# A two-layer attention and convolution trunk: attention turns one step later behind the scores, four score buffers, and one weight unit in another slot

## The chip, the cores and the metric

The kernel runs on one core of a Trainium2 chip, in one launch, in float32 with split products (below). The metric is the device time of the launch in microseconds. Before the change it is 2429.41 us, the median of three runs (2428.79 to 2430.34).

## The reference

Two layers, each on a residual stream x of 1024 positions by 1024 channels:

```
h    = rmsnorm(x);  proj = h @ w_in
q, k, v, conv_in = split(proj)            # 8 heads of 64; 512 + 512 convolution columns
q, k = rope(rmsnorm(q)), rope(rmsnorm(k))
attn = mixture of 3 dilated sliding windows (128/1, 512/4, 2048/16), causal, softmax weights joined
u    = a * sigmoid(g)                     # a, g from conv_in
u    = silu(layernorm(causal depthwise conv, 31 taps))
x    = x + concat(attn, u) @ w_out
h    = rmsnorm(x);  up = causal depthwise conv of 3 taps over (h @ w_up)
x    = x + (silu(gate) * value) @ w_down  # 2816 hidden channels
```

The three windows are joined into one softmax: each score gets the logarithm of how many windows hold that key (the table `logcount`), so attention is one causal softmax per head.

## The kernel before

Data lies transposed, channels on partitions. Every large product is made of three: high parts of weight and operand, and the two cross terms with the low parts (`split_product`). A *unit* is 1024x128 weights against all 1024 positions: 48 matmuls of 128x512. A unit's weights arrive in `w_raw[0]` or `w_raw[1]` (by parity); ScalarE writes the high part (`hi`, L793), VectorE the low part (`lo`, L1105), into a numbered pair of `w_hi` and `w_lo`. Pairs 0 to 2 are buffers of their own; pair 3 is `q_first` and `k_hh_first`, which the attention stage uses for queries and keys and the feed-forward stage for weights.

The work of one layer, in order: twenty units of the input projection (0 and 1: first group of q; then convolution value, gate, and two of q or k in turns; last four of v), the attention stage, the output projection, the feed-forward part. TensorE, ScalarE and VectorE each have an order written out by hand; semaphores join them.

**The third unit.** Units 0 and 1 go into slots 0 and 1. Unit 2 goes into slot 0 again, so its high part is written only after unit 0 has been read out of the accumulator: `qk_read` copies `mm[0]` (L852), squares it (L853, which releases the accumulator), and then calls `hi` for unit 2; VectorE's `lo(0, 2)` follows, and TensorE waits for it (`weights_split`) at the start of unit 2.

**The taps.** The 31-tap convolution is done on VectorE in 192 half-length instructions (`tap`, mostly L1191) in a fixed order that `tap_schedule` deals out to named slots between other work: for pass i over a q or k group ahead of the value (`value`), ahead of the gate (`gate`), ahead of the norm, under the rope, and under the reading. What is left over (53 instructions) goes into the attention steps, one in each step but the fourth of every head (`TAPS_AT`).

**The attention stage.** A step n is one block of 128 queries of one head: 8 heads of 8 steps, the blocks in the order `BLOCKS = (0, 6, 1, 7, 2, 4, 3, 5)` (a block b has b+1 key blocks). For step n:
- TensorE makes the scores into `mm[n % 2]` (`scores`, L596); it waits until the scores of step n-2 have been read.
- VectorE adds the table, finds the row maximum and writes `sc[n % 3]` (`add_mask`, L1321), then mostly one tap.
- ScalarE takes the exponential in place (`exps`, L926).
- Two steps later TensorE transposes the blocks, up to four at a time, into one of three *turn banks* in rotation (`turn`, kind "p", L623); ScalarE copies each out (`read_turn`, L940), which frees the bank.
- TensorE multiplies with v in four groups per head (`attend`, L642), pair 0 (6 instructions in the trace), pair 3 (30), pair 1 (14), pair 2 (22), at steps 5, 7, 9 and 11 after the head's first; those with an odd index stand ahead of the step's turns.
- ScalarE moves the result out (`move_out`, L949), TensorE turns it back (kind "h", at step 14), VectorE divides by the row sums (`read_out`, L1339 and L1341).
- For each pair of heads the finished columns are turned in two halves (kind "o", steps 24 and 26), read by ScalarE into `x_hi` (L943) and by VectorE into `x_lo` (L1331). Only this second read frees the bank.

In a step ScalarE first reads that step's "p" turns, then takes its exponential, then reads "o" turns. VectorE does mask, tap, "o" read, `read_out`. With positions in the head counted from 0, TensorE's order is: 0: scores, turn of 6; 1: scores, turn of 7, pair 1; 2: scores, turn of 0; 3: scores, pair 2, turn of 1; 4: scores, turn of 2; 5: scores, turn of 3, pair 0; 6: scores, turn of 4, "h"; 7: scores, pair 3, turn of 5. "o" turns end positions 0 and 2 of every second head.

After step 64 no scores are left; the tail (to `LAST_STEP`) finishes the last head, with four parts of the first output unit between. The GpSimd engine adds the four convolution tiles (L1515) as each one's last tap is done.

## Time and profile before

| what | us |
|---|---|
| median of three runs | 2429.41 |
| the profiled execution | 2427.01 |
| its span | 2425.2 |
| TensorE busy (PE) | 2377.7 (98%) |
| VectorE busy (DVE) | 1547.7 (64%) |
| ScalarE busy (ACT) | 790.5 (33%) |
| GpSimd busy (POOL) | 157.0 (6%) |
| DMA over the span | 63 GB/s |
| TensorE's granted clock | 1.00 of full speed in every window read |

All times in the rows are microseconds from the start of the span. Busy time of TensorE counts from a matmul's start to its modelled end, and neighbours overlap; a wait shown before an instruction begins only at that modelled end. The two layers lie 1204 us apart and show the same picture; rows are of the first. In it the input projection runs to about 251, attention to about 396, the output projection to about 480.

### The profile page before, as it was taken

The numbers are of one execution on the slowest core, as the hardware profiler recorded it, in microseconds if no ns is written. First come the engines' busy times: TensorE is split into PE (matmuls) and PEld (weight loads), VectorE is DVE, ScalarE is ACT, GpSimd is POOL, SyncE is SP. The second block draws the span as 40 slices with busy tenths as digits, with TensorE's granted clock in tenths as the row PEclk, the third lists the DMA queues.
The fourth block names the chain that finished last, engine by engine and source line by source line (L and its number), as shares of the span: only waits on it lengthen the run. The fifth ranks groups of instructions, "written<-read, shape, count | busy, mean of one in ns | idle before, by whom it ended". The sixth has DMA issues, their size and how long they took to land.

```text
span 2425.2 us, 30715 instructions
## 1 busy us (share of the span) xinstructions
PE 2377.7 (98%) x11672; PEld 1945.6 (80%) x11672; DVE 1547.7 (64%) x1659; ACT 790.5 (33%) x1050; POOL 157.0 (6%) x57
## 2 busy tenths in 40 slices
PE   7999999999999999999999998999999999999999
PEld 6888777888888888888778887778888888888887
DVE  5999774665555555555749997756555555555555
ACT  4322674432222222222332227754322222222221
POOL 0122001100000000000102120011000000000000
PEclk9999999999999999999999999999999999999999
DMA  4323531121111111111112244301211111111111
GB/s 159 88 79 114 144 81 36 44 61 52 35 52 52 52 43 52 43 52 43 43 35 79 79 139 114 79 18 53 61 53 44 48 39 52 52 51 44 46 49 70
DMA packets 46676, 153.44 MB, mean 63 GB/s; under 512 B 7424, under 2 KB 10112, under 8 KB 46592
## 3 DMA queue, kind: packets, MB, share of 16 engines
q1 hardware_dynamic: 45728, 149.93, 21.3%
q10 hardware_dynamic: 864, 2.36, 0.2%
q8 instruction: 57, 0.93, 0.2%
q14 instruction: 27, 0.22, 0.0%
HBM read 131.02 MB, written 21.23 MB: 63 GB/s over the span
## 4 chain that ended last, share of the span: by engine, by line
PE 88%; issue 5%; DVE 3%; ACT 2%; POOLq 0%; DMA 0%; DVEq 0%; POOL 0%; SPq 0%; ACTq 0%
PE mm L484 60%; PE aux L484 20%; PE aux L642 3%; PE aux L623 2%; PE mm L596 2%; PE aux L511 1%; DVE y L1191 1%; ACT sc L926 1%; ACT pT_large L940 0%; PE aux L520 0%; DMA x<-xT 0%; POOLq L1499 0%; DVE x_lo L1117 0%; PE aux L577 0%; DVE w_lo L1105 0%
## 5 line engine op out<-in xcount | busy, mean ns | idle before, releaser
L484 PE MATMUL mm<-x_hi,w_hi 128*128 128x512 f32 x1952 | 609.4, 393 | 17.5 <-DVE x_lo L1117 11.5
L484 PE MATMUL mm<-x_hi,w_lo 128*128 128x512 f32 x1952 | 604.5, 391 | 0.0
L484 PE MATMUL mm<-x_lo,w_hi 128*128 128x512 f32 x1952 | 604.1, 391 | 0.0
L484 PEld LDWEIGHTS mm<-x_hi,w_hi 128*128 128x128 f32 x1952 | 363.9, 188 | 97.0 <-issue 12.4
L484 PEld LDWEIGHTS mm<-x_lo,w_hi 128*128 128x128 f32 x1952 | 366.9, 188 | 79.6
L484 PEld LDWEIGHTS mm<-x_hi,w_lo 128*128 128x128 f32 x1952 | 366.7, 188 | 79.0
L793 ACT ACTIVATE w_hi<-w_raw 128x1024 fp32r<-128x1024 f32 x154 | 161.9, 1058 | 659.1 <-PE mm L484 461.2
L1111 DVE TENSOR_TENSOR x<-x,aux 128x1024 f32<-128x1024 f32 x176 | 214.8, 1221 | 121.2 <-PE aux L484 111.6
L1105 DVE TENSOR_TENSOR w_lo<-w_raw,w_hi 128x1024 fp32r<-128x1024 f32 x154 | 196.6, 1282 | 54.0 <-ACT w_hi L793 50.0
L1123 DVE TENSOR_TENSOR uv<-mm,rinv 128x1024 f32<-128x1024 f32 x44 | 53.9, 1225 | 220.3 <-PE mm L484 220.1
L1191 DVE SCALAR_TENSOR_TENSOR y<-u_all,cpar,y 128x512 f32<-128x512 f32 x248 | 186.6, 765 | 0.1
L1123 DVE TENSOR_TENSOR ug<-mm,rinv 128x1024 f32<-128x1024 f32 x44 | 53.9, 1225 | 181.3 <-PE mm L484 158.8
L1321 DVE CUSTOM_DVE_ANT_0 sc<-mm,logcount 128x128 f32<-128x128 f32 (+7 forms) x128 | 96.3, 756 | 57.0 <-PE mm L596 28.6
L484 PE MATMUL mm<-x_hi,q_first 128*128 128x512 f32 x352 | 111.1, 397 | 0.0
L484 PE MATMUL mm<-x_lo,q_first 128*128 128x512 f32 x352 | 111.0, 396 | 0.0
L484 PE MATMUL mm<-x_hi,k_hh_first 128*128 128x512 f32 x352 | 110.9, 396 | 0.0
L926 ACT ACTIVATE sc<-sc,small 128x128 f32<-128x128 f32 (+7 forms) x128 | 99.5, 777 | 18.3 <-DVE small L1321 16.7
L484 PE MATMUL aux<-h_hi_odd,w_hi 128*128 128x512 f32 x320 | 101.0, 397 | 0.0
L484 PE MATMUL aux<-h_lo_odd,w_hi 128*128 128x512 f32 x320 | 100.9, 396 | 0.0
L484 PE MATMUL aux<-h_hi_odd,w_lo 128*128 128x512 f32 x320 | 100.9, 396 | 0.0
L1191 DVE SCALAR_TENSOR_TENSOR y<-u_all,taps_sum,y 128x512 f32<-128x512 f32 x120 | 98.0, 817 | 2.6 <-ACT y L846 1.8
L623 PE MATMUL aux<-ident,sc 128*128 128x128 f32 x576 | 86.0, 277 | 13.6 <-ACT sc L926 11.8
(190 smaller groups left out, 2938.9 us busy)
## 6 DMA issues: line engine op xcount, KB each, us to landing
w_raw<-weights SPq DMA_DIRECT2D x188, 512.0 KB, 3.6
qk_scratch<-m SPq DMA_DIRECT2D x64, 128.0 KB, 2.1
qk_scratch<-o SPq DMA_DIRECT2D x64, 128.0 KB, 2.1
x_hi<-qk_scratch SPq DMA_DIRECT2D x32, 256.0 KB, 6.4
q_first<-qk_scratch SPq DMA_DIRECT2D x8, 512.0 KB, 4.6
k_hh_first<-qk_scratch SPq DMA_DIRECT2D x16, 256.0 KB, 6.0
k_ll_first<-qk_scratch SPq DMA_DIRECT2D x16, 256.0 KB, 6.5
x_hi<-qk_scratch SPq DMA_DIRECT2D x8, 512.0 KB, 4.8
```

Source lines behind the costliest of these rows:

```text
L484: last = pe.matmul(acc[:, cols], a, b[:, cols], start=start and n == 0, stop=stop and n == 2)
L511: last = pe.matmul(stat_s[:, b * n:(b + 1) * n], src[:, b * P:(b + 1) * P], rhs, start=src is sources[0], stop=src is sources[-1])
L596: last = pe.matmul(mm[n % 2][:, a:z], q_st[b][:, qb * P:(qb + 1) * P], k[b][:, a:z], start=k is k_hh, stop=k is k_ll)
L623: last = pe.transpose(bank[:, c * P:(c + 1) * P], block_, ident[:])
L642: last = pe.matmul(o_bank[half * HEAD_DIM:(half + 1) * HEAD_DIM, cols], vp[b][:, kb, hh * HEAD_DIM:(hh + 1) * HEAD_DIM], pT(h * TB + BLOCK ...
L793: act.activation(w_hi[slot][:], w_raw[raw][:], ACT.Copy).then_inc(w_hi_ready, 1)
L926: act.activation(s, s, ACT.Exp, bias=neg_max[:, n % 4:n % 4 + 1], scale=-1.0, accum_out=row_sum[:, h % 2, qb:qb + 1]).then_inc(exp_done, 1)
L1105: dve.tensor_tensor(w_lo[slot][:], w_raw[base % 2][:], w_hi[slot][:].bitcast(F32), ALU.subtract).then_inc(weights_split, 1)
L1111: dve.tensor_tensor(t, t, buf[:], ALU.add).then_inc(read, 1)
L1123: dve.tensor_tensor(dst, mm[buf][:], rinv[:], ALU.mult).then_inc(mm_read, 1)
L1191: op = dve.scalar_tensor_tensor(y_odd if kind == "odd" else y_even, src[:, i:i + HALF_SEQ], par, y_odd if kind == "odd" and i else y_even, ...
L1321: dve.tensor_tensor_reduce(sc[n % 3][:, 0:keys], mm[n % 2][:, 0:keys], logcount[:, SEQ - keys:SEQ], -SCALE, 3e38, ALU.add, ALU.min, neg_ma ...
```

## The change

- Turns (kind "p") come three steps behind their scores, no longer two. The four `attend` groups, `move_out`, the "h" and the "o" turns move by one step with them, so they keep their places relative to the turns; the stage has 76 steps in place of 75. Only the scores now run one step further ahead. TensorE's order by position in the head becomes: 0: scores, pair 3, turn of 5; 1: scores, turn of 6, first "o"; 2: scores, turn of 7, pair 1; 3: scores, turn of 0, second "o"; 4: scores, pair 2, turn of 1; 5: scores, turn of 2; 6: scores, turn of 3, pair 0; 7: scores, turn of 4, "h".
- Four score buffers `sc[n % 4]` in place of three, cut to the widest block each has to hold, so they fit into the same memory. The wait for the stores of q and k moves with the first use of the fourth.
- VectorE reads the "o" turns of a step one step later, after the next step's mask and tap; the "h" turn it reads in its own step, as before.
- Unit 2 uses pair 3. ScalarE writes its high part right after the splitting of x (in the second layer after a wait for the last down-projection, which reads pair 3), VectorE its low part at the head of its next list; the `hi` inside the first `qk_read` is left out.
- In the second pass (i = 1) 20 taps in place of 15 stand ahead of the gate and none in place of 4 under the rope; 52 in place of 53 are left for the steps.

```diff
@@ -74,11 +74,11 @@
 SQ_ADDS = KT // 2 - 1
 QK_STORES = 16 * 4 * HPT * QKG
 STEPS = HEADS * TB
-O_AT = 24
-H_AT = 14
+O_AT = 25
+H_AT = 15
 BLOCKS = (0, 6, 1, 7, 2, 4, 3, 5)
-ATTENDS = ((5, 0, 2), (7, 3, 3), (9, 1, 6), (11, 2, 7))
-LAST_STEP = STEPS + 11
+ATTENDS = ((6, 0, 2), (8, 3, 3), (10, 1, 6), (12, 2, 7))
+LAST_STEP = STEPS + 12
 DOWN = GROUPS * KT
 X_UPD = 2 * KT + DOWN
 C_PAR = TAPS + 3
@@ -109,9 +109,9 @@
     slots = {"own": (0,) * 6}
     for i in range(CT - 1):
         tiles = (i, i - 1) if i else (i, i)
-        slots[i, "value"], slots[i, "gate"] = (tiles * 4)[:7], (tiles * 8)[:15 if i == 1 else 9]
+        slots[i, "value"], slots[i, "gate"] = (tiles * 4)[:7], (tiles * 10)[:20 if i == 1 else 9]
         slots[i, "norm"] = (tiles * 4)[:8 if i == 2 else 0]
-        slots[i, "rope"], slots[i, "read"] = (i + 1, i) * 2, (i + 1, i) * 5
+        slots[i, "rope"], slots[i, "read"] = (i + 1, i) * (0 if i == 1 else 2), (i + 1, i) * 5
     slots["v0"], slots["v1"], slots["v2"] = (CT - 1, CT - 2) * 4, ((CT - 1, CT - 2) * 7)[:13], (0, 1) * 4
     chain = tap_chain()
     done = [sum(tiles.count(c) for tiles in slots.values()) for c in range(CT)]
@@ -144,10 +144,10 @@
 
     fills = []
     for n in range(LAST_STEP):
-        if 2 <= n < STEPS + 2:
-            qb = BLOCKS[(n - 2) % TB]
+        if 3 <= n < STEPS + 3:
+            qb = BLOCKS[(n - 3) % TB]
             for a in range(0, qb + 1, 4):
-                fills.append((n, "p", n - 2, a, min(a + 4, qb + 1)))
+                fills.append((n, "p", n - 3, a, min(a + 4, qb + 1)))
         if n >= H_AT and (n - H_AT) % TB == 0 and n < STEPS + H_AT:
             fills.append((n, "h", (n - H_AT) // TB, None, None))
         for half in range(2):
@@ -239,7 +239,8 @@
         pT_large = sb("pT_large", [P, 2 * TB, P], to=attn)
         pT_small = cos[:].rearrange("p (k q) -> p k q", q=P)
         o_turned = [sin[:, i * BANK:(i + 1) * BANK] for i in range(2)]
-        sc = [sb(f"sc{i}", [P, SEQ], to=attn) for i in (2, 0, 1)]
+        widest = [(max(BLOCKS[i], BLOCKS[i + 4]) + 1) * P for i in range(4)]
+        sc = [sb(f"sc{i}", [P, widest[i]], to=attn) for i in (3, 0, 1, 2)]
         sc = sc[1:] + sc[:1]
         v_home = [sa[:], sb_[:], v_third[:], v_fourth[:]]
         vp = [v.rearrange("p (b c) -> p b c", b=TB) for v in v_home]
@@ -548,7 +549,7 @@
                             last.then_inc(mm_full, 1)
 
                 first_units()
-                unit(0, 0, 2, 2, midway=lambda: spread(o2, 0, 0))
+                unit(3, 0, 2, 2, midway=lambda: spread(o2, 0, 0))
                 unit(1, 1, 3, 3)
 
                 for i in range(QKG - 1):
@@ -610,7 +611,7 @@
 
                             pe.wait_ge(statb_read, at(l, STAT_B, B_MEAN + 1))
                         pe.wait_ge(exp_done, at(l, STEPS, which + 1))
-                        blocks = [sc[which % 3][:, kb * P:(kb + 1) * P] for kb in range(a, z)]
+                        blocks = [sc[which % 4][:, kb * P:(kb + 1) * P] for kb in range(a, z)]
                     elif kind == "h":
 
                         pe.wait_ge(o_moved, at(l, HEADS, which + 1))
@@ -657,10 +658,10 @@
                         last.then_inc(mm_full, 1)
 
                 for n in range(LAST_STEP):
-                    if n == STEPS + 4:
+                    if n == STEPS + 5:
                         pe.wait_ge(o_split, at(l, 2 * PAIRS, 2 * PAIRS - 2))
                         out_part(0, 0, [0], 0)
-                    if n == STEPS + 7:
+                    if n == STEPS + 8:
                         out_part(0, 0, [1], 0)
                     if n < STEPS:
                         scores(n)
@@ -832,6 +833,9 @@
                         hi(1, 1)
                     split_x(0, t, 0)
                     square(0, t, squares1)
+                if l:
+                    act.wait_ge(down_full, l * DOWN)
+                hi(3, 2)
 
                 def read_rinv(b0):
                     act.wait_ge(statb_full, at(l, STAT_B, b0 + 1))
@@ -851,7 +855,8 @@
                     unit_done(mbase + half, 4, i)
                     act.activation((ta, tg)[half][:], mm[half][:], ACT.Copy)
                     act.activation((sa, sb_)[half][:], mm[half][:], ACT.Square).then_inc(qk_copied, 1)
-                    hi(half, mbase + half + 2, 4, i)
+                    if mbase or half:
+                        hi(half, mbase + half + 2, 4, i)
 
                 def qk_norm(i):
                     small_mean(TB * HPT, S_QK, HEAD_DIM, 1, i, eps=0.0)
@@ -918,7 +923,7 @@
 
                 def exps(n):
                     h, qb = n // TB, BLOCKS[n % TB]
-                    s = sc[n % 3][:, 0:(qb + 1) * P]
+                    s = sc[n % 4][:, 0:(qb + 1) * P]
                     act.wait_ge(mm_read, at(l, MM, M_SCORE + n + 3))
                     if n % TB == 0:
 
@@ -951,8 +956,8 @@
 
                 for n in range(LAST_STEP):
 
-                    if n >= 11 and (n - 11) % TB == 0 and n < STEPS + 11:
-                        move_out((n - 11) // TB)
+                    if n >= 12 and (n - 12) % TB == 0 and n < STEPS + 12:
+                        move_out((n - 12) // TB)
                     for f in range(PT):
                         if FILLS[f][0] == n and FILLS[f][1] == "p":
                             read_turn(f)
@@ -1244,7 +1249,7 @@
                     dve.wait_ge(qk_copied, at(l, 2 * QKG, 2 * g + 2))
                     dve.sem_inc(mm_read, 2)
 
-                lo(0, 2)
+                lo(3, 2)
                 lo(1, 3)
                 if l == 0:
                     rope_angles()
@@ -1311,14 +1316,14 @@
 
                     keys = (BLOCKS[n % TB] + 1) * P
                     dve.wait_ge(mm_full, at(l, MM, M_SCORE + n + 1))
-                    if n == 2:
+                    if n == 3:
 
                         dve.wait_ge(qk_stored, at(l, QK_STORES, QK_STORES + 16))
-                    if n >= 3:
-
-                        dve.wait_ge(pt_full, at(l, PT, LAST_FILL[n - 3] + 1))
+                    if n >= 4:
+
+                        dve.wait_ge(pt_full, at(l, PT, LAST_FILL[n - 4] + 1))
                     plain(dve)
-                    dve.tensor_tensor_reduce(sc[n % 3][:, 0:keys], mm[n % 2][:, 0:keys],
+                    dve.tensor_tensor_reduce(sc[n % 4][:, 0:keys], mm[n % 2][:, 0:keys],
                                              logcount[:, SEQ - keys:SEQ], -SCALE, 3e38, ALU.add, ALU.min,
                                              neg_max[:, n % 4:n % 4 + 1]).then_inc(mm_read, 1)
 
@@ -1346,7 +1351,7 @@
 
                 step_taps = list(STEP_TAPS)
 
-                for n in range(LAST_STEP):
+                for n in range(LAST_STEP + 1):
                     if n < STEPS:
                         add_mask(n)
                         if n == 3:
@@ -1354,7 +1359,7 @@
                         for _ in range(min(TAPS_AT[n % TB], len(step_taps))):
                             tap(step_taps.pop(0))
                     for f in range(PT):
-                        if FILLS[f][0] == n:
+                        if FILLS[f][0] == n - 1:
                             read_turn(f)
                     if n >= H_AT and (n - H_AT) % TB == 0 and n < STEPS + H_AT:
                         read_out((n - H_AT) // TB)
```

## Rows read from the trace of the kernel before

**Rows 1.** Waits of TensorE, 254 to 388 us: us in total, times, longest.
```profile
PE aux L623 <- ACT sc L926: 5.9, 9, 1.3
PE mm L596 <- DVE small L1321: 4.1, 7, 1.4
```

**Rows 2.** Windows by head: length, busy us (count) per engine, clock, DMA share, GB/s.
```profile
250.62:264.84 14.22, 10.72 (x70) 8.35 (x70) 10.66 (x22) 11.72 (x24) 0.00 (x0) 1.00 0.64 149
...
280.63:296.42 15.79, 15.08 (x138) 12.36 (x140) 11.83 (x26) 11.87 (x30) 0.06 (x1) 1.00 0.43 101
296.42:315.14 18.72, 16.62 (x147) 13.27 (x148) 14.70 (x28) 12.89 (x32) 2.38 (x1) 1.00 0.35 86
315.14:330.94 15.80, 15.08 (x138) 12.36 (x140) 11.44 (x26) 11.86 (x30) 0.00 (x0) 1.00 0.43 101
330.94:348.41 17.47, 16.38 (x146) 13.34 (x148) 12.78 (x28) 12.88 (x32) 0.00 (x0) 1.00 0.39 91
...
381.67:396.83 15.16, 13.34 (x116) 10.62 (x116) 3.60 (x7) 5.05 (x12) 0.00 (x0) 1.00 0.22 57
```

**Rows 3.** Timeline, attention: start, us, instruction, in brackets the idle time before it.
```profile
256.63 0.50 PE L596 MATMUL mm<-k_hh_first,q_first 128*128 128x512 f32 x1 [1.37 <-DVE small L1321]
...
291.26 1.15 ACT L926 ACTIVATE sc<-sc,small 128x1024 f32<-128x1024 f32 x1
...
292.64 1.07 PE L623 MATMUL aux<-ident,sc 128*128 128x128 f32 x8 [0.57 <-ACT sc L926]
...
304.18 1.20 PE L596 MATMUL mm<-x_hi 128*128 128x512 f32 x4 [0.35 <-DVE small L1321]
...
310.00 0.96 PE L596 MATMUL mm<-x_hi 128*128 128x512 f32 x4 [1.07 <-DVE small L1321]
...
386.02 0.85 PE L623 MATMUL aux<-ident,sc 128*128 128x128 f32 x6 [1.31 <-ACT sc L926]
```

**Rows 4.** Timeline at the third unit, first layer.
```profile
35.90 1.02 ACT L853 ACTIVATE sa<-mm 128x1024 f32<-128x1024 f32 x1
...
37.06 0.61 PE L484 MATMUL mm<-x_hi,w_lo 128*128 128x512 f32 x2
...
37.89 1.23 DVE L1105 TENSOR_TENSOR w_lo<-w_raw,w_hi 128x1024 fp32r<-128x1024 f32 x1 [6.64 <-ACT w_hi L793]
...
39.17 0.73 PE L484 MATMUL mm<-x_hi,w_hi 128*128 128x512 f32 x2 [1.50 <-DVE w_lo L1105]
```

**Rows 5.** Timeline and chain (start, us, what), second and third pass.
```profile
132.10 1.22 DVE L1128 TENSOR_TENSOR o<-mm,rinv 128x1024 f32<-128x1024 f32 x1 [0.33 <-PE mm L484]
...
132.87 32.66 PE mm L484 x144
...
147.60 1.06 ACT L793 ACTIVATE w_hi<-w_raw 128x1024 fp32r<-128x1024 f32 x1
...
178.35 1.23 DVE L1128 TENSOR_TENSOR o<-mm,rinv 128x1024 f32<-128x1024 f32 x1 [4.46 <-PE mm L484]
...
202.42 0.72 PE L484 MATMUL mm<-x_hi,w_hi 128*128 128x512 f32 x2 [1.51 <-DVE w_lo L1105]
```

**Rows 6.** Timeline of GpSimd and VectorE at the second tile sum.
```profile
304.87 2.38 POOL L1515 TENSOR_TENSOR u_all<-u_all,y 128x1024 f32<-128x1024 f32 x1 [24.17 <-DVE y L1191]
...
305.04 2.75 DVE L1191 SCALAR_TENSOR_TENSOR y<-u_all,cpar,y 128x512 f32<-128x512 f32 x1
```

**Rows 7.** Timeline: one instruction of each kind around a turn bank.
```profile
285.75 1.09 PE L642 MATMUL aux<-cos,sa 128*64 128x128 f32 x14
...
287.50 0.42 DVE L1321 CUSTOM_DVE_ANT_0 sc<-mm,logcount 128x256 f32<-128x256 f32 x1 [0.68 <-PE aux L623]
...
287.85 0.74 DVE L1191 SCALAR_TENSOR_TENSOR y<-u_all,cpar,y 128x512 f32<-128x512 f32 x1
...
301.38 0.60 ACT L943 ACTIVATE x_hi<-aux 128x512 fp32r<-128x512 f32 x1
...
302.01 0.69 DVE L1331 TENSOR_TENSOR x_lo<-aux,x_hi 128x512 fp32r<-128x512 f32 x1 [1.58 <-ACT x_hi L943]
```

## The prediction, made before the changed kernel had run

> **What bounds the kernel now.** I read the windows by head first, then TensorE's waits, then the timeline at each wait. TensorE is busy 98% of the span, so only what makes it idle, or its own work, counts. The change adds and removes no matmul: both versions make the same scores, turns and products. It can win only idle time of TensorE. That lies in two places it touches.
>
> In attention a head without "o" turns takes 15.79 us with 15.08 busy; the reader is to see that the same head later takes 15.80. There are four such heads between the start and the tail (the window at 280.63 and its like). Two heads with "o" turns take 17.47 with 16.38 busy, a third 18.72 with 16.62. The start of the stage has 3.50 idle of 14.22, the tail 1.82 of 15.16 [rows 2]. TensorE waited 5.9 us for exponentials and 4.1 us for masks [rows 1]. So about 12.5 us per layer are idle, and no more can be won there without hidden gaps.
>
> In the input projection TensorE waits 1.50 us for the low part of the third unit's weights [rows 4] and 1.51 us at the seventeenth unit [rows 5].
>
> **Third unit.** Now the chain is: square of unit 0 ends at 35.90 + 1.02 = 36.92, high part, low part at 37.89, ends 39.12, unit 2 at 39.17. Unit 1's last matmuls end at 37.06 + 0.61 = 37.67 [rows 4]. With the weights in pair 3, written while ScalarE and VectorE wait (VectorE idles 6.64 us just there), only the square stands ahead: 36.92, which is 0.75 before 37.67. The 1.50 goes whole. Next in line is unit 3, a full unit later, and its high part comes about a microsecond earlier, since one ScalarE instruction of 1.06 ahead of it is gone. What comes earlier in DMA is the load of unit 4's weights, into a free raw buffer. Gain 1.5 per layer. Bounds: 0 (something else holds unit 2) and 1.5.
>
> Does the lead survive? VectorE is in step with TensorE from the gate of the first pass on, so it moves along. The wait at the seventeenth unit (1.51) is VectorE's own chain of 24.07 us from the gate at 178.35 to 202.42 [rows 5]; the third pass has the same taps after the change, so this wait stays and moves with the rest.
>
> **Second pass.** Five more taps ahead of the gate: 5 x 0.66 (the 0.74 of a tap overlaps its neighbour by 0.08) = 3.3, less the 0.33 that VectorE waited there [rows 5]: the gate read, the norm and the rope come 3.0 later. Behind them ScalarE's rounding, its reading of unit 10 and the high part of unit 12 move too: from 147.60 + 1.06 to 151.7. The four taps dropped under the rope would have covered that; VectorE now idles about 1.5 there, and the low part ends at about 152.9. TensorE needs it two thirds into the piece of 32.66 us at 132.87 that is units 10 to 12 [rows 5], so at 132.87 + 21.8 = 154.6. 1.7 us are left. VectorE enters the third pass about 2.1 us later, and 4.46 idle are there ahead of the next gate [rows 5]. Cost and gain nothing; if the cover fails, each microsecond beyond 1.7 is paid twice (two layers). Bounds: 0 to a loss of 2 per layer.
>
> **Attention, heads without "o".** The largest wait is for the exponential of block 7: it ends at 291.26 + 1.15 = 292.41, its turn begins at 292.64 after 0.57 idle [rows 3]. With the turn one step later, TensorE has the scores of the next step and two transposes more in front of it, over a microsecond. The wait goes. Also the lengths of steps get more even: pair 3 (1.9) now stands between short scores, so a mask has two steps of 1 to 3 us in which to finish. I went through TensorE's order with the rows' durations, VectorE and ScalarE beside it. Every mask is ready over 1 us ahead of the scores that need its accumulator. What is late next is ScalarE, which after the long exponential has the move, two reads and another exponential, and finishes the read of block 2's turn about when pair 0 wants it (0 to 0.3). ScalarE is busy 12 of 15.8 [rows 2]. I take 15.1: 0.7 x 4 = 2.8. Bounds: 0 and 4 x 0.9, the idle time and some hidden under the modelled ends.
>
> **Heads with "o".** VectorE idles 1.58 for ScalarE ahead of the "o" read [rows 7]; the mask behind it is late and TensorE waits 0.35 for it at the next wide scores [rows 3]. One step later in VectorE's list this goes. The added wait is on the other side: the turn bank is freed only after the next mask and tap. From the end of the first "o" turn, VectorE still has about 1.25 of the long mask and tap, then 0.42, 0.74, 0.69 and a drain of some 0.3: 3.35. TensorE has scores 0.35, a turn 0.75, pair 1 (1.09), scores 1.1: 3.2 [rows 3, 7] until the turn that takes this bank. So 0.1 to 0.3 of waiting, twice per such head. Behind it in TensorE's queue stand all later scores. I take 16.5 for the 17.47: 0.95 x 2 = 1.9. Bounds: a loss of 1 and a gain of 1.5 each.
>
> The third such head has GpSimd's sum: it runs 304.87 to 307.25 and a tap takes 2.75 in place of 0.74 [rows 6, 7]; TensorE then waits 1.07 for a mask [rows 3]. The last tap of that tile moves one place forward, into the step of block 0, so the sum falls where VectorE waits for the long scores. The extra 1.25 over the other heads may stay or go; I take half, so 18.72 becomes 17.1: 1.6.
>
> The Trainium skill ("SBUF — State Buffer", section on the two separate sides) says that VectorE and GpSimd share one port pair, held by whichever starts first for its whole instruction, and that a VectorE instruction is caught by it only in a two-port mode or with two SBUF inputs. The trace agrees, 2.75 against 0.74 for a tap with two such inputs. By that rule the mask, which reads PSUM, runs beside the sum, only the tap's last 0.6 or so is lost, and this head would come to 16.9 in place of 17.1; by the row alone nothing says that the mask is spared.
>
> **Start and tail.** At the start nothing is there to fill TensorE; the 1.37 for the first wide mask stays [rows 3], and the 1.06 for an exponential gives back about 0.4, as one more scores step is done by then. In the tail the turn of the last step waits 1.31 [rows 3]; afterwards pair 3 and two turns lie ahead of it (over 3 us against some 2.3 for mask and exponential). 1.0 goes, 0.3 comes back on banks. The extra step has no work of its own. The qk-store wait moves to the fourth mask; nothing was late there.
>
> Sum per layer: 1.5 + 2.8 + 1.9 + 1.6 + 1.0 + 0.4 = 9.2, both layers 18.4. The profiled execution took 2427.01 (span 2425.2 and 1.8 around it); it becomes 2408.6. The median of the runs shown lies 2.4 above the profiled one, so 2411.0.
>
> **The rivals.** All are told apart from no change at about 0.2%, 4.9 us.
>
> *Half of it.* The waits for exponentials go, but TensorE, arriving earlier, meets ScalarE's reads and the banks: of 7.7 per layer in attention 3.8 is won. For it: ScalarE has 12 to 13 us of work in heads of 15 to 16 [rows 2], in one order, so each late mask delays reads behind it. Against: it idles over 2 us in each head before the turns after pair 3. Or the second pass takes 2 per layer. 2411.0 + 7.7 = 2418.7.
>
> *Slower.* The "o" turns' bank. Place: VectorE's read after the next mask and tap, eight halves per layer, sixteen in all. If VectorE runs late as a whole, because heads get shorter and its 11 to 13 us of work stay, the bank comes free d later each time. It decides at 18.4 / 16 = 1.15 us each; at 1.6 each the time is 2411 + 25.6 = 2436.6. For it: masks wait in VectorE's list behind taps. Against: it has 2.7 to 5 us idle in each head.
>
> *Only the third unit.* The attention period is set by something the rows don't show, and moving the turns only moves the same idle time: 3.0 won, 2426.4, the same within the bound.
>
> **How the numbers follow.** The forecast has 0.65, half of it 0.23, only the third unit 0.06, slower 0.06. Faster is the first two, 0.88; same 0.06; slower 0.06. The range: the forecast's own bounds (hidden gaps won, bank waits nothing) reach down to 2403; up it goes into the half case, to 2421, leaving out the rest of that case and the two others.
>
> **What would show it.** In the profile after: the idle of 1.50 at unit 2 gone and that of 1.51 at the seventeenth unit still there; no wait of a turn on an exponential between the first and last head; heads of 15.1 and 16.5; small waits for the "o" read's drain or ScalarE's reads in their place. It would be wrong if heads stay at 15.8, if a wait of a microsecond appears at the turn of block 0 or 2, or if unit 12 waits for its weights.

## The result, and the profile after

The changed kernel takes 2402.19 us (median; 2402.05 to 2402.47), the kernel before in the same set of runs 2429.1 (2427.03 to 2430.34): a ratio of 0.9892, 95% interval 0.988 to 0.9905. The profiled execution took 2402.06 us, its span 2400.3, against 2427.01 and 2425.2. So 26.9 us by the medians and 24.95 by the two profiled executions. The direction was right; the forecast of 2411.0 gave only two thirds of the gain, and the time lies 0.8 us below the stated range.

The page's line of busy time, and the windows by head in the first layer (columns as in [rows 2]; these windows, too, begin where pair 3's products begin):

```profile
PE 2370.7 (99%) x11672; PEld 1945.4 (81%) x11672; DVE 1546.4 (64%) x1659; ACT 788.6 (33%) x1050; POOL 162.0 (7%) x57
```

```profile
249.00:262.62 13.62, 10.78 (x70) 8.58 (x68) 11.31 (x23) 11.62 (x23) 0.00 (x0) 1.00 0.65 156
262.62:278.49 15.87, 15.03 (x138) 12.41 (x137) 12.78 (x24) 12.15 (x32) 2.38 (x1) 1.00 0.44 100
278.49:293.21 14.72, 14.72 (x138) 12.42 (x137) 11.31 (x26) 11.72 (x30) 0.00 (x0) 1.00 0.48 109
293.21:309.29 16.08, 15.79 (x145) 13.21 (x144) 13.22 (x28) 12.89 (x32) 2.38 (x1) 1.00 0.42 99
...
324.01:339.76 15.75, 15.75 (x145) 13.23 (x144) 12.70 (x28) 12.78 (x32) 0.00 (x0) 1.00 0.41 101
...
369.99:382.68 12.69, 12.02 (x113) 10.01 (x112) 3.57 (x8) 5.15 (x11) 0.00 (x0) 1.00 0.14 42
```

The reader is to see that in the third and fifth of these rows TensorE is now busy for the whole window: 14.72 of 14.72 where it was 15.08 of 15.79 [rows 2], and 15.75 of 15.75 where it was 16.38 of 17.47. The same instructions also count fewer busy microseconds. What is left is in the first head from pair 3 on (0.84 idle, second row), the third (0.29, fourth row), and at both ends of the stage (first and last row).

Where the time came from, in us by the same events in both traces (the first layer's, then the second's):

| stretch | before | after | won | forecast |
|---|---|---|---|---|
| first square sum to the last transpose of v | 221.41, 222.66 | 219.88, 221.16 | 1.53, 1.50 | 1.5 |
| from there to pair 3 of head 0 | 11.85, 11.46 | 11.36, 11.34 | 0.49, 0.12 | 0.4 |
| heads, pair 3 of head 0 to pair 3 of head 7 | 116.84, 116.85 | 107.37, 107.37 | 9.47, 9.48 | 6.3 |
| from there to the square sum of the feed-forward | 118.20, 118.20 | 117.06, 117.08 | 1.14, 1.12 | 1.0 |

TensorE's waits in the projection and attention, first layer (start, length, instruction, idle before it):

```profile
200.77 0.73 PE L485 MATMUL mm<-x_hi,w_hi 128*128 128x512 f32 x2 [1.47 <-DVE w_lo L1110]
...
254.62 0.50 PE L597 MATMUL mm<-k_hh_first,q_first 128*128 128x512 f32 x1 [1.12 <-DVE small L1326]
...
259.04 0.50 PE L597 MATMUL mm<-k_hh_first,q_first 128*128 128x512 f32 x1 [0.42 <-DVE small L1326]
...
274.66 1.09 PE L624 MATMUL aux<-ident,sc 128*128 128x128 f32 x8 [0.59 <-ACT pT_large L945]
...
276.00 0.66 PE L643 MATMUL aux<-cos,sa 128*64 128x128 f32 x6 [0.25 <-ACT cos L945]
...
301.01 0.33 PE L624 MATMUL aux<-ident,sc 128*128 128x128 f32 x1 [0.29 <-DVEq L1338]
```

The wait of 1.50 at the third unit [rows 4] is gone (37 to 49 us is busy throughout), that of 1.51 at the seventeenth [rows 5] is still there with 1.47 (first row above), and no turn between the first head and the last waits for an exponential.

The second pass and the gate of the third, VectorE:

```profile
149.99 1.23 DVE L1110 TENSOR_TENSOR w_lo<-w_raw,w_hi 128x1024 fp32r<-128x1024 f32 x1 [1.54 <-ACT w_hi L794]
...
176.75 1.22 DVE L1133 TENSOR_TENSOR o<-mm,rinv 128x1024 f32<-128x1024 f32 x1 [2.76 <-PE mm L485]
```

It idles 1.54 for the high part of unit 12 (1.5 was forecast) and still 2.76 ahead of the gate (4.46 before), so TensorE loses nothing there.

The new waits of 0.59 and 0.25 come from GpSimd's first tile sum:

```profile
268.29 2.38 POOL L1520 TENSOR_TENSOR u_all<-y 128x1024 f32<-128x1024 f32 x1 [47.75 <-DVE y L1196]
```

```profile
268.47 2.75 DVE L1196 SCALAR_TENSOR_TENSOR y<-u_all,cpar,y 128x512 f32<-128x512 f32 x1
271.14 1.21 DVE L1326 CUSTOM_DVE_ANT_0 sc<-mm,logcount 128x1024 f32<-128x1024 f32 x1
...
272.39 1.16 ACT L931 ACTIVATE sc<-sc,small 128x1024 f32<-128x1024 f32 x1 [2.27 <-DVE small L1326]
```

The sum holds up a tap (2.75 where a tap alone takes 0.74) just ahead of the widest mask; ScalarE idles 2.27, and its reads of the turns are late when TensorE wants them. With the sums moved out of the heads, in an experiment below, both waits are gone.

### The profile page after: what moved, and what is told of

It is laid out like the page before. It is cut to its first block, busy times and chain, and to the rows that moved or that the text cites. A ratio compares the mean times of both kernels' runs of the same rounds, so it can differ in the third digit from the quotient of the medians.

```text
span 2400.3 us, 30716 instructions
## 1 busy us (share of the span) xinstructions
PE 2370.7 (99%) x11672; PEld 1945.4 (81%) x11672; DVE 1546.4 (64%) x1659; ACT 788.6 (33%) x1050; POOL 162.0 (7%) x57
## 4 chain that ended last, share of the span: by engine, by line
PE 90%; issue 4%; DVE 4%; ACT 1%; DVEq 0%; POOLq 0%; DMA 0%; POOL 0%; SPq 0%; ACTq 0%
PE mm L485 60%; PE aux L485 20%; PE aux L643 3%; PE aux L624 3%; PE mm L597 3%; PE aux L512 1%; DVE y L1196 1%; DVE x_lo L1122 1%; PE aux L521 0%; DMA x<-xT 0%; POOLq L1504 0%; DVE sc L1326 0%; PE aux L578 0%; DVE w_lo L1110 0%; DVE o L1245 0%
## 5 line engine op out<-in xcount | busy, mean ns | idle before, releaser
L485 PE MATMUL mm<-x_hi,w_hi 128*128 128x512 f32 x1920 | 598.7, 393 | 14.3 <-DVE x_lo L1122 11.3
L485 PE MATMUL mm<-x_hi,w_lo 128*128 128x512 f32 x1920 | 594.6, 391 | 0.0
L485 PE MATMUL mm<-x_lo,w_hi 128*128 128x512 f32 x1920 | 594.1, 391 | 0.0
L485 PEld LDWEIGHTS mm<-x_lo,w_hi 128*128 128x128 f32 x1920 | 360.7, 188 | 78.3
L485 PEld LDWEIGHTS mm<-x_hi,w_lo 128*128 128x128 f32 x1920 | 360.7, 188 | 77.6
L1110 DVE TENSOR_TENSOR w_lo<-w_raw,w_hi 128x1024 fp32r<-128x1024 f32 x152 | 190.3, 1257 | 54.5 <-ACT w_hi L794 50.7
L1326 DVE CUSTOM_DVE_ANT_0 sc<-mm,logcount 128x128 f32<-128x128 f32 (+7 forms) x128 | 95.7, 755 | 46.6 <-PE mm L597 26.9
L485 PE MATMUL mm<-x_hi,q_first 128*128 128x512 f32 x384 | 121.4, 397 | 0.0
L485 PE MATMUL mm<-x_lo,q_first 128*128 128x512 f32 x384 | 121.0, 396 | 0.0
L485 PE MATMUL mm<-x_hi,k_hh_first 128*128 128x512 f32 x384 | 120.9, 396 | 0.0
L1038 ACT ACTIVATE cg<-cg 128x1024 f32<-128x1024 f32 x44 | 46.7, 1062 | 128.5 <-DVE cg L1444 128.5
```

The costliest lines, as they stand in the source:

```text
L485: last = pe.matmul(acc[:, cols], a, b[:, cols], start=start and n == 0, stop=stop and n == 2)
L1038: act.activation(cg[:], cg[:], ACT.Silu).then_inc(gate_ready, 1)
L1110: dve.tensor_tensor(w_lo[slot][:], w_raw[base % 2][:], w_hi[slot][:].bitcast(F32), ALU.subtract).then_inc(weights_split, 1)
L1326: dve.tensor_tensor_reduce(sc[n % 4][:, 0:keys], mm[n % 2][:, 0:keys], logcount[:, SEQ - keys:SEQ], -SCALE, 3e38, ALU.add, ALU.min, neg_ma ...
```

## The experiments

The theory after the result: between the start and the tail of the stage, TensorE's own work in a head is 14.72 us, 15.75 with "o" turns, and the change takes away every wait above it but those that GpSimd's sums cause. The rivals: VectorE still sets the pace; the fourth buffer or the later "o" read is not needed; the moved taps keep the lead of the third unit. Each ratio below is to the kernel before, run on the same chip (its medians there were 2426.83, 2427.18 and 2427.14 in the three sets).

### The third unit alone

```diff
-                unit(0, 0, 2, 2, midway=lambda: spread(o2, 0, 0))
+                unit(3, 0, 2, 2, midway=lambda: spread(o2, 0, 0))
...
+                if l:
+                    act.wait_ge(down_full, l * DOWN)
+                hi(3, 2)
...
-                    hi(half, mbase + half + 2, 4, i)
+                    if mbase or half:
+                        hi(half, mbase + half + 2, 4, i)
...
-                lo(0, 2)
+                lo(3, 2)
```

> The kernel before with only the third in-projection unit moved to pair 3. Theory (the parts add up): 1.65 us per layer, the shift seen at the seventeenth unit in the two traces, so 3.3 us less than before in both the span and the timed runs, and no change in attention. Rival (the lead needs the moved taps): VectorE gives the lead back in the second pass, and the span is less than 1 us below before.

Measured 2425.74 us (2423.85 to 2427.59), ratio 0.9992, interval 0.9983 to 1.0001: the times alone don't settle it. The trace does: from the first square sum (33.46) to the last transpose of v (253.37) 219.91 us, as in the changed kernel and 1.50 less than before (1.43 less in the second layer); heads of 15.79 and 17.47, as before. The span falls by only 1.1 because the first square sum comes 1.95 later in this trace than in the one before (31.51). The 1.65 expected was read from shifts that hold a difference at the start, 0.13 of it. The rival is out: the lead doesn't need the moved taps.

### The attention part alone

The changed kernel with the third unit's edit (the diff above, in reverse) and that of the taps undone:

```diff
-        ... (tiles * 10)[:20 if i == 1 else 9]
+        ... (tiles * 8)[:15 if i == 1 else 9]
...
-                unit(3, 0, 2, 2, midway=lambda: spread(o2, 0, 0))
+                unit(0, 0, 2, 2, midway=lambda: spread(o2, 0, 0))
```

> The kernel before with only the attention part of the change: turns three steps behind, four buffers, the o read one step later. Theory (TensorE's own work is the floor): 24.95 less the 3.3 of the third unit, so 21.6 us less span than before, heads without o turns at 14.7 us, with them at 15.5 to 16.1. Rival (the parts need each other): less than 18 us, with waits for masks left in the heads. GpSimd's two early sums fall on other taps than in the changed kernel, which may move 1 us per layer either way.

2407.96 us (2405.93 to 2408.65), ratio 0.992, interval 0.9906 to 0.9933; span 2406.0, 19.2 less. Heads without "o" take 14.71 (the second 14.8), with 15.74 (once 15.97), as in the changed kernel. The 21.6 expected was 2.4 too much. The loss is in the third head, of 17.56 and 19.15 us against 16.08 and 16.09, where GpSimd's second sum falls; a part comes back in the first head, which takes 14.71 against 15.87, as the first sum falls elsewhere.

### The taps of the second pass put back

```diff
-        slots[i, "value"], slots[i, "gate"] = (tiles * 4)[:7], (tiles * 10)[:20 if i == 1 else 9]
+        slots[i, "value"], slots[i, "gate"] = (tiles * 4)[:7], (tiles * 8)[:15 if i == 1 else 9]
...
-        slots[i, "rope"], slots[i, "read"] = (i + 1, i) * (0 if i == 1 else 2), (i + 1, i) * 5
+        slots[i, "rope"], slots[i, "read"] = (i + 1, i) * 2, (i + 1, i) * 5
```

> The changed kernel with the taps of the second pass dealt as before (15 ahead of the gate, 4 under the rope). Theory (VectorE's slack covers both deals): in-projection equal to 0.2 us, and only the place of GpSimd's sums differs, within 1 us per layer. Rival (the moved taps keep the lead of the third unit): a new wait of TensorE in the second or third pass and 1.5 us per layer lost.

2405.24 us (2403.29 to 2405.58), ratio 0.9907, interval 0.9892 to 0.9922, about 2 to 3 above the changed kernel. The projection is 219.89, equal to 0.01. The third head takes 19.18 in the first layer and 17.55 in the second, against 16.09 in the changed kernel. The rows of the first layer's:

```profile
298.54 2.38 POOL L1520 TENSOR_TENSOR u_all<-u_all,y 128x1024 f32<-128x1024 f32 x1 [20.25 <-DVE y L1196]
298.72 0.08 DVE L1326 DVE_READ_ACCUMULATOR2_ANT small<- 128x1 f32 x1
298.72 2.75 DVE L1196 SCALAR_TENSOR_TENSOR y<-u_all,cpar,y 128x512 f32<-128x512 f32 x1
...
301.39 0.68 DVE L1336 TENSOR_TENSOR x_lo<-aux,x_hi 128x512 fp32r<-128x512 f32 x1
302.17 0.33 PE L624 MATMUL aux<-ident,sc 128*128 128x128 f32 x1 [1.77 <-DVEq L1338]
```

The tap held by the sum now stands right ahead of the "o" read, and TensorE waits 1.77 for that read's bank. In the changed kernel, with one tap less left for the steps, the last tap of the third tile falls a step earlier and the wait is 0.29. The moved taps have a price too: with them back the first sum no longer holds up the first head, which takes 14.69 and 14.71 against 15.87. Over pair 3 of head 0 to pair 3 of head 7 the moved taps win 2.0 us in the first layer and 0.6 in the second, and nothing in the pass they were moved in.

### The "o" read back in its own step

```diff
-                for n in range(LAST_STEP + 1):
+                for n in range(LAST_STEP):
...
-                        if FILLS[f][0] == n - 1:
+                        if FILLS[f][0] == n:
```

> The changed kernel with VectorE's o read back in its own step, ahead of the next mask. Theory (masks now have over 1 us to spare): heads with o turns stay at 15.75 us, the time within 1 us of the changed kernel. Rival (this reordering is what frees those heads): each of the three heads with o turns gets back 0.35 to 0.7 us of waiting for masks, 2 to 4 us in all.

2411.37 us (2411.28 to 2412.77), ratio 0.9937, interval 0.9923 to 0.995: 9.2 above the changed kernel, the rival's side and over twice its size. Heads with "o" take 17.28 to 17.41 in the first layer:

```profile
325.47:342.77 17.30, 16.37 (x145) 13.29 (x144) 12.70 (x28) 12.79 (x32) 0.00 (x0) 1.00 0.40 92
```

```profile
305.90 0.44 PE L624 MATMUL aux<-ident,sc 128*128 128x128 f32 x2 [0.53 <-DVEq L1338]
...
306.74 0.73 PE L597 MATMUL mm<-x_hi 128*128 128x512 f32 x2 [0.40 <-DVE small L1326]
```

The window is the fifth head's, the rows are the third's; the fifth has the same two waits of 0.53 and 0.40. They make 0.93, and the head is 1.55 longer. The rest is in busy time: 16.37 against 15.75 for the same work. Two masks in each such head, those of blocks 1 and 2, have lost what they had to spare: in the changed kernel they end 1.9 to 2.0 and 2.3 us ahead of the scores that need their accumulator, here both 0.06.

### Three score buffers

```diff
-        sc = [sb(f"sc{i}", [P, widest[i]], to=attn) for i in (3, 0, 1, 2)]
+        sc = [sb(f"sc{i}", [P, SEQ], to=attn) for i in (2, 0, 1)]
...
-                    if n >= 4:
+                    if n >= 3:
-                        dve.wait_ge(pt_full, at(l, PT, LAST_FILL[n - 4] + 1))
+                        dve.wait_ge(pt_full, at(l, PT, LAST_FILL[n - 3] + 1))
```

(and `% 3` for `% 4` where the buffers are named, the wait for the stores at step 2.)

> The changed kernel with three score buffers, turns still three steps behind: a mask then waits for the turns of the step three before, which TensorE does in the same step behind its scores. Theory (masks have over 1 us to spare ahead of the scores that need them): heads without o turns stay within 0.3 us of 14.72, the time within 4 us of the changed kernel, so the fourth buffer is worth little. Rival (the buffer is what lets the scores run ahead): heads go back to over 15.5 us and the time to over 2412 us.

2414.82 us (2414.52 to 2415.47), ratio 0.9949, interval 0.9932 to 0.9966. Both expectations were half right: heads without "o" stay at 14.86 from the second on, those with it go to 17.71 (the third to 18.44, with a sum of GpSimd's in it).

```profile
312.82:327.67 14.85, 14.85 (x138) 12.47 (x137) 11.32 (x26) 11.65 (x30) 0.00 (x0) 1.00 0.48 108
327.67:345.38 17.71, 16.03 (x146) 13.23 (x145) 12.70 (x28) 12.98 (x32) 0.00 (x0) 1.00 0.39 90
```

```profile
302.90 0.33 PE L623 MATMUL aux<-ident,sc 128*128 128x128 f32 x1 [1.00 <-DVEq L1337]
...
305.53 0.98 PE L623 MATMUL aux<-ident,sc 128*128 128x128 f32 x7
...
306.69 0.56 DVE L1325 CUSTOM_DVE_ANT_0 sc<-mm,logcount 128x384 f32<-128x384 f32 x1 [2.05 <-issue]
...
307.84 0.68 DVE L1335 TENSOR_TENSOR x_lo<-aux,x_hi 128x512 fp32r<-128x512 f32 x1
...
308.62 0.44 PE L623 MATMUL aux<-ident,sc 128*128 128x128 f32 x2 [1.42 <-DVEq L1337]
```

A mask must now wait for the turns of the step three before, which stand behind its own scores: the one at 306.69 begins only behind those of 305.53, which end at 306.51. The "o" read stands behind the mask (307.84), so its bank comes 0.27 to 1.42 late for the turn at 308.62 and its like. This is the mechanism of the rival "slower" in the prediction, at the place it named; the fourth buffer is what keeps it away.

### The taps out of the steps

```diff
-                        for _ in range(min(TAPS_AT[n % TB], len(step_taps))):
-                            tap(step_taps.pop(0))
...
+                for n in step_taps:
+                    tap(n)
```

> The changed kernel with the 52 convolution taps of each layer's attention steps done after the steps (the stage's end then waits for them, so the whole time says nothing; some 30 us per layer more). It takes 4.6 us per head off VectorE. Theory (14.72 and 15.75 us are TensorE's own work in a head): the heads keep these times to 0.05 us, the first becomes 14.72 too as GpSimd's sum is no longer there. Rival (VectorE still sets the pace): heads get shorter by 0.3 us or more.

```profile
263.23:277.92 14.69, 14.69 (x137) 12.43 (x137) 6.21 (x17) 12.03 (x32) 0.00 (x0) 1.00 0.46 108
277.92:292.65 14.73, 14.73 (x138) 12.43 (x137) 6.67 (x19) 11.70 (x30) 0.00 (x0) 1.00 0.43 108
292.65:308.39 15.74, 15.74 (x145) 13.23 (x145) 8.16 (x21) 12.78 (x32) 0.00 (x0) 1.00 0.43 102
```

VectorE falls from 11.3 to 6.7 us per head and the head stays at 14.7, so VectorE doesn't set the pace. No instruction of TensorE in these heads shows a wait. Summed from start to start in the second head, the scores take 5.58 us here and in the changed kernel, the turns 4.17, the products with v 4.98 and 4.97; before the change it was 6.59, 4.23 and 4.97. So 14.72 is TensorE's own work in this order. ScalarE's work was not taken off in any run; that it doesn't set the pace either is read from the missing waits. (The whole took 2488.38 us in its one execution, as the taps then stand alone.)

### The later "o" read alone, on the kernel before

```diff
-                for n in range(LAST_STEP):
+                for n in range(LAST_STEP + 1):
...
-                        if FILLS[f][0] == n:
+                        if FILLS[f][0] == n - 1:
```

> The kernel before with only one thing changed: VectorE reads an o turn after the next step's mask and tap. Theory (in heads with o turns VectorE's stall behind ScalarE is a loss of its own): these heads fall from 17.47 to about 16.7, those without stay at 15.79, some 5 us in all. Rival (without the third step the later release of the bank only moves the wait): heads with o turns stay within 0.2 us of 17.47.

2423.11 us (2422.44 to 2423.99), ratio 0.9981, interval 0.9971 to 0.999. Heads with "o" fall to 17.23 (from 17.47, and the third from 18.72), those without stay at 15.79:

```profile
313.77:329.56 15.79, 15.08 (x137) 12.36 (x136) 11.43 (x26) 11.86 (x30) 0.00 (x0) 1.00 0.39 101
329.56:346.79 17.23, 16.08 (x145) 13.30 (x144) 12.69 (x28) 12.86 (x32) 0.00 (x0) 1.00 0.42 93
```

```profile
304.04 0.33 PE L623 MATMUL aux<-ident,sc 128*128 128x128 f32 x1 [0.57 <-DVEq L1333]
```

In between the two expectations. A wait of 0.57 for the bank takes the place of those for masks. Most of the 4.1 us won is in the third head, the one with GpSimd's second sum: 1.48 in each layer. In the other heads with "o" the later read is worth 0.24 without the third step, the third step 0.17 without the later read (17.47 to 17.30), and both 1.72.

### GpSimd's sums after the last tap

```diff
-                    pool.wait_ge(tap_done, at(l, N_TAPS, TAP_LAST[c] + 1))
+                    pool.wait_ge(tap_done, at(l, N_TAPS, TAP_LAST[CT - 1] + 1))
```

> The changed kernel with GpSimd's three tile sums all done after the last tap. Theory (the sums block one tap each, and the first two reach TensorE): the first head falls from 15.87 to 14.72 and the third from 16.08 to 15.75, 1.48 us per layer, 3.0 in all, so about 2399.2 us; the end of the stage doesn't wait for the sums. Rival (three sums in a row, 7.2 us, come late for the mean of the layer norm): the stage's end moves out by more than 1.5 us per layer and the time is the same or more.

2399.69 us (2398.96 to 2400.7), ratio 0.9888, interval 0.9872 to 0.9905. The theory is met to 0.5 us, and the stage's end doesn't move out (117.04 us from pair 3 of head 7 to the square sum of the feed-forward, 117.07 in the changed kernel):

```profile
262.65:277.36 14.71, 14.71 (x138) 12.43 (x137) 10.86 (x24) 12.19 (x32) 0.00 (x0) 1.00 0.48 108
...
292.08:307.81 15.73, 15.73 (x145) 13.22 (x144) 12.70 (x28) 12.75 (x32) 0.00 (x0) 1.00 0.42 103
```

### That, and three taps of the third pass ahead of the gate

```diff
-        ... (tiles * 10)[:20 if i == 1 else 9]
-        slots[i, "norm"] = (tiles * 4)[:8 if i == 2 else 0]
+        ... (tiles * 10)[:(9, 20, 12)[i]]
+        slots[i, "norm"] = (tiles * 4)[:5 if i == 2 else 0]
```

> The changed kernel with GpSimd's sums after the last tap and, in the third pass, three taps moved from ahead of the norm to ahead of the gate (12 and 5 in place of 9 and 8), where VectorE idled 2.4 to 4.5 us. Theory (the seventeenth unit waits for VectorE's chain from the gate on): that chain is 2.0 us shorter, the wait of 1.47 us goes in each layer, 2.9 us less than with the late sums alone, about 2396.5 us. Rival (the norm of q or k then waits for its own inputs, or VectorE's work up to the attention stage decides): the wait moves to the end of the projection and less than 1 us per layer is won.

2395.5 us (2395.22 to 2395.73), ratio 0.9867, interval 0.9851 to 0.9884. The wait at the seventeenth unit is gone, TensorE runs on into it, and VectorE still idles ahead of the gate; the projection is 1.77 us shorter in each layer than in the changed kernel:

```profile
177.05 1.22 DVE L1133 TENSOR_TENSOR o<-mm,rinv 128x1024 f32<-128x1024 f32 x1 [0.81 <-PE mm L485]
```

```profile
177.82 32.66 PE mm L485 x144
```

### And the 22nd unit's weights at steps 7 and 8

```diff
-                    if n == 2:
+                    if n == 7:
                         hi(1, U_V + 5)
...
-                        if n == 3:
-                            lo(1, U_V + 5)
...
+                        if n == 8:
+                            lo(1, U_V + 5)
```

> The same, with the 22nd unit's high and low part made at steps 7 and 8 of the first head in place of 2 and 3. Theory (in the first steps VectorE's low part delays the mask of step 4): the wait of 0.42 us at the scores of step 6 goes, 0.4 to 0.8 us per layer, and nothing is lost in the head behind. Rival (it lands in the second head): the head at steps 8 to 16 grows from 14.72 us by as much as is won.

2395.28 us (2395.11 to 2396.36), ratio 0.9868, interval 0.9852 to 0.9885: not told apart from the last. The wait of 0.42 goes and one of 0.24 for ScalarE's read comes at 258.51; the second head stays at 14.73. Neither expectation came true: nothing is lost in the second head, and only 0.05 is won per layer up to pair 3 of head 0. These last two are the fastest versions, 31.6 and 31.9 us below the kernel before.

### The changed kernel again, with no edit

> The changed kernel again, beside its variants on one chip. Theory: 2402.2 us as before, with both start and heads the same to 0.1 us; what differs from run to run is the arrival of x at the start. Rival: it shows other modes of a few us, as the kernel before does (2426.4 to 2430).

2403.05 us (2402.36 to 2403.84), ratio 0.9898, interval 0.9881 to 0.9914. In its trace the first square sum comes at 33.25, 1.87 later than in the first (31.38), and every stretch behind it is the same to 0.1. So the time by which these two traces differ was lost before that sum, while x arrives; why it arrives later was not tried. That the other runs differ for the same reason is not shown.

## Why the prediction fell short

**The step that failed** is the size of a head: "I take 15.1: 0.7 x 4" and "I take 16.5 for the 17.47: 0.95 x 2". They are 14.72 and 15.75. Over all heads from pair 3 of head 0 to pair 3 of head 7, 6.3 us per layer were forecast and 9.5 measured. Of the 3.2 missed, 0.4 is in the four heads without "o" (3.2 won for 2.8, nothing of it in the first), 1.0 in the third head (2.6 won for 1.6), and 1.8 in the other two with "o" (3.7 won for 1.9). Two errors made it.

First, I took TensorE's busy time as the least a head can take (15.08, and 16.38 with "o"). It is not: before, such a head showed 0.71 idle and lost 1.07. The same instructions were busy 15.08 before, 14.72 after, and 14.73 with 40% of VectorE's work gone, so busy time holds lost time. These rows show where. The first two are of the kernel before, ahead of its turn at 292.64 [rows 3]; the others are of the changed kernel, where nothing waits:

```profile
284.45 0.39 PE L596 MATMUL mm<-k_ll_first,q_first 128*128 128x512 f32 x1
...
291.79 0.28 PE L596 MATMUL mm<-k_ll_first,q_first 128*128 128x256 f32 x1
```

```profile
281.69 0.39 PE L597 MATMUL mm<-k_ll_first,q_first 128*128 128x512 f32 x1
281.92 0.60 PE L624 MATMUL aux<-ident,sc 128*128 128x128 f32 x4
...
292.00 0.28 PE L597 MATMUL mm<-k_ll_first,q_first 128*128 128x256 f32 x1
292.12 0.49 PE L624 MATMUL aux<-ident,sc 128*128 128x128 f32 x3
```

Where nothing waits, the turn starts 0.12 behind the start of the 256-wide score product, though that product is recorded as 0.28 long. Before, it started 0.85 behind: 0.73 were lost, and 0.57 shown as idle. The other product, 512 wide, was followed at 284.98, 0.53 behind its start in place of 0.23: 0.30 were lost, and 0.14 shown. So each wait hides its first 0.16 us under the recorded end, and these two make 1.03 of the 1.07 lost. The Trainium skill ("Perfetto Trace Analysis", section on the per-engine timelines, Tensor Engine Instruction) says that TensorE's end times are estimated from an instruction's size, not observed; these rows agree with that. I had put these hidden gaps into the range ("some hidden under the modelled ends") and not into the value.

For heads with "o" it is the larger error: my 16.5 is just above the busy time of 16.38, and the same work takes 15.75.

Second, in heads with "o" I counted 0.1 to 0.3 of bank wait twice from a race of 3.35 against 3.2 (the terms listed add up to 3.40 and 3.29). It shows only where GpSimd's sum falls (0.29), and not in the others. The 0.3 for a drain was too much: in the changed kernel's third head VectorE's read ends at 300.91 and the turn that takes the bank starts at 301.01, 0.10 later.

**The 2.4 added at the end** was wrong too. I lifted the result by the difference between the median shown (2429.41) and the profiled execution (2427.01), as if it belonged to the kernel. In its 35 later runs, in three sets, the kernel before had medians of 2426.8 to 2427.2. Without it the forecast is 2408.6, the range 2.4 lower, and the time inside it; but the heads are the larger part, 6.4 of the 8.8.

**What held.** The third unit: 1.5 forecast, 1.53 and 1.50 measured, and the seventeenth unit's wait stayed. The second pass: no cost in the projection, with idle times of 1.54 and 2.76 for about 1.5 and 2.4 forecast. Start and tail together: 1.4 forecast, 1.6 and 1.2 measured. From the second head's window on (278.49) every mask ends at least 0.98 us ahead of the scores that need its accumulator, about as forecast (over 1 us). The danger named for the "o" turns' bank was real: with three buffers it comes true.

**What I missed.** GpSimd's first sum, which cost nothing before, falls behind the tap of position 2 in the first head and costs 1.15 us per layer (15.87 against 14.72); and the moved taps, priced at nothing, decide where both sums fall. The second sum itself did less harm, as these rows of the changed kernel show (GpSimd's, then VectorE's, of the third head):

```profile
296.37 2.38 POOL L1520 TENSOR_TENSOR u_all<-u_all,y 128x1024 f32<-128x1024 f32 x1 [25.70 <-DVE y L1196]
```

```profile
297.01 1.09 DVE L1326 CUSTOM_DVE_ANT_0 sc<-mm,logcount 128x896 f32<-128x896 f32 x1 [0.72 <-PE mm L597]
298.03 0.08 DVE L1326 DVE_READ_ACCUMULATOR2_ANT small<- 128x1 f32 x1
298.03 1.27 DVE L1196 SCALAR_TENSOR_TENSOR y<-u_all,cpar,y 128x512 f32<-128x512 f32 x1
```

The mask, with one input in PSUM, ran beside the sum at its usual length (1.09, as in the first head of the changed kernel at 266.44, with no sum running), and the tap took 1.27 in place of 2.75, its loss being the sum's last 0.5. So the Trainium skill's rule on the shared port pair ("SBUF — State Buffer", section on the two separate sides), with which the prediction weighed 16.9 for this head against 17.1, held: the head is 16.08, 0.33 above the others with "o", where the prediction had 0.4 by the rule and 0.6 without it.

## What to carry to other kernels

Where a wait lies between two engines in a pipelined loop, take the floor of the bound engine from starts of instructions that follow each other without a stall, not from its busy time. Two edits that each win 0.2 can win 1.7 together, if each alone leaves the other's wait in place: try both before dropping either. When work moves by a step, look again at what an engine off the path does at that moment.

## What the runs showed of the hardware

TensorE's wait of 1.77 us for the "o" read is in both layers of two traces, the attention part alone and the taps put back. In two of the four cases its granted clock fell afterwards to half. The windows behind the wait in one of them (the taps put back, first layer):

```profile
302.00:304.00 2.00, 1.83 (x15) 1.46 (x17) 1.68 (x4) 0.62 (x2) 0.00 (x0) 0.86 0.00 0
304.00:306.00 2.00, 2.00 (x18) 1.72 (x15) 1.45 (x4) 1.38 (x3) 0.00 (x0) 0.50 0.00 0
306.00:309.00 3.00, 3.00 (x20) 2.73 (x20) 0.79 (x2) 2.45 (x6) 0.00 (x0) 0.86 0.00 0
```

Here 0.50 of full speed is 1.2 GHz, and 1.00 is 2.4. Pair 2's 22 products took 2.78 us at that clock, and 1.53 with the attention part alone, where the same wait of 1.77 left the clock at 1.00. The third head was 17.56 and 17.55 us where the clock stayed, 19.15 and 19.18 where it fell: 1.6 us more for the same stall. What decides between the two is not shown. The shorter waits of 1 to 1.5 us elsewhere in these traces were followed by no fall.
